# Sparse attention with four buffers; memory keys, part of the memory values and the convolution's norm inside its loop; all convolution taps ahead of the rotary step

## The chip, the cores and the metric

One core of one Trainium2 chip. The metric is the device time of one launch in microseconds. TensorE is called PE below, VectorE DVE, ScalarE ACT, GpSimd POOL, and SyncE, which starts most weight transfers, SP.

## The reference, cut to what matters

A first block (pooling and gated mixers, then latent attention) gives x, 512 tokens by 1024 features. The second block, on x and on 256 memory tokens, is:

```python
# h = rmsnorm(x); z = h @ w_in, split into a, b, q, k/v pairs and gate logits
u = a * sigmoid(b)                            # 512 channels
y = depthwise_conv(u, 31 taps, causal) + bias
conv = silu(layernorm(y))                     # 512 features
q_r, k_s, k_w = rotary of the first 16 of 64 dimensions
# 8 heads, 2 key groups; three branches, each with its own gate:
o_cmp = softmax(q . compressed keys) @ compressed values      # 31 blocks
o_slc = causal softmax(q_r . k_s) @ v_s       # all blocks are selected at 512 tokens
o_win = causal softmax(q_r . k_w) @ v_w       # the window is 512 tokens
x = x + concat(conv, g0*o_cmp + g1*o_slc + g2*o_win) @ w_out
mem_n = rmsnorm(mem)                          # 256 tokens
k = mem_n @ w_mem_k;  v = mem_n @ w_mem_v;  q = rmsnorm(x) @ w_mem_q
x = x + softmax(q . k / 16) @ v @ w_mem_o     # 4 heads
x = final_rmsnorm(x + peer(rmsnorm(x)))       # 128 gathered expert rows per token
```

## The kernel before, in words

Every engine runs one instruction list written out by hand, and the lists meet at semaphores. Activations lie feature-major (128 features on the partitions, tokens along a row). All is fp32. PSUM's eight banks are handed out ahead of time: each use of a bank is a job, `claim` waits for the bank's earlier use to be read out (`freed`), `done` and `full` tell that a result stands in it. Weights come in blocks of 1024 by 512 (2 MB) through a ring of three slots. SP walks the list `BLOCKS` (L39) in order and loads block b once block b-3 was released by PE (L452 to L475).

The change touches the stage of sparse attention and what lies around it, in this order on PE:

- Input projection (L786 to L807), block by block. Before the last two token tiles of its fifth block PE makes six products for the rotary step (L798, L801). DVE works on the convolution meanwhile: 124 instructions, 31 taps for each of 4 channel tiles (`conv_taps`, L1641; `CACC` is the sum). It does 92 of them (L1666), then the rotary step (L1669 to L1677: three instructions for each of six tiles, which frees six banks), and spreads the other 32 over the loop below (L1733).
- Compressed keys and values (L809 to L827). Their jobs take the banks that the rotary step frees. L830 waits for all six rotary tiles before the loop begins.
- The loop of sparse attention, 64 items: 8 heads, 4 query tiles `qt`, 2 branches. An item is 128 queries by (qt+1)*128 keys. PE makes the scores (`scores2`, L859, 64 rows of the array in use), DVE adds the mask, takes the maximum and its negative into `SM` (`masked_max`, L1706), ACT takes the exponential into `P2` (L1257), DVE divides by the sum and multiplies by the gate (`normalise`, L1578, its last instruction L1587), PE transposes (`transpose2`, L869), ACT copies out to `PT2` (L1263), and PE multiplies by the values (`values2`, L878). `SM`, `P2` and `PT2` have two buffers. Each head also has a small compressed branch (L832 to L857, L1678 to L1704).

The order in the loop before, per item i:

```python
PE:  scores2(i + 2); transpose2(i); values2(i - 1)
DVE: normalise(i); masked_max(i + 2); one convolution tap in 3 of 4 items
ACT: exp(i); copy_out(i - 1)
```

- In the loop ACT squares the memory tokens (item 4), PE sums them (item 10), and DVE scales them into `MEMT` (items 16 to 23).
- After the loop PE sums the convolution's channels (L914), makes the memory keys from `MEMT` in two blocks of 32 products of 256 columns (L917 to L921), with the sum of squares for the convolution's variance between them (L923), and waits for `mix_conv`: the SiLU of the normed convolution (L924, L1283 to L1286 on ACT), for which DVE centers, inverts and scales (L1753 to L1756).
- Then the output projection `out2` (L931), the memory values in two blocks of 16 products of 512 columns (L933 to L941), the memory queries, memory attention, and the expert stage, which gathers 512 rows of 8 KB per partition and takes the second half of the time.

Of the kernel before, what the change touches and what calls it, by code (L numbers as in the profile page):

```python
# [19 lines left out]
KC = D // P  # L20
# [7 lines left out]
TAPS = 31  # L28
# [11 lines left out]
          ("mem_k", 2), ("out2", 2), ("mem_v", 2), ("mem_q", 2), ("mem_o", 2), ("peer_q", 4)]  # L40
# [50 lines left out]
def build(nc, a, out):  # L91
# [8 lines left out]
    with ctx:  # L100
# [104 lines left out]
        SM = area(80, 2, L)  # L205
# [10 lines left out]
        P2 = area(72, 2, L)  # L216
        PT2 = area(76, 2, L)
        SB2 = area(169, 4, L)
        SQ2 = area(72, 4, L)
# [8 lines left out]
        MV = area(120, 2, D)  # L228
        MQ = area(128, KC, L)
# [169 lines left out]
        for hh in range(8):  # L399
            if hh % 2 == 0:  # L400
                j_o2[hh // 2] = J.take(6 + (hh // 2) % 2)
            j_cs[hh] = J.take(5)
            j_cpt[hh] = J.take(5)
            if hh == 1:
                j_rms_mem = [J.take(5)]
            for m in range(8):
                j_s2[8 * hh + m] = J.take((8 * hh + m) % 3)
                j_pt2[8 * hh + m] = J.take(3 + (8 * hh + m) % 2)
        J.align()
        j_ln_cv = [J.turn(1)]  # L410
        j_mk = J.turn(4)
        j_ln_cv.append(J.turn(1))
        j_mk += J.turn(4)
        j_rms_mq = J.turn(1)
        j_out2 = J.turn(8, [j_rms_mq[0][0]])
        j_mv = J.turn(4)
# [68 lines left out]
        def _(pe):  # L485
# [383 lines left out]
            def transpose2(i):  # L869
                hh, qt, br = ITEMS2[i]  # L870
                j = j_pt2[i]
                claim(pe, j)
                pe.wait_ge(S["p_ready"], N1 + i + 1)
                for kt in range(qt + 1):
                    ins = nc.tensor.transpose(bank(j, P, kt * P), P2[:, i % 2, kt * P:(kt + 1) * P], ident[:, :])  # L875
                done(ins, j)

            def values2(i):  # L878
                hh, qt, br = ITEMS2[i]
                jj, g = HEAD2[hh]  # L880
                jo = j_o2[hh // 2]
                read_out(pe, [j_pt2[i]])
                for kt in range(qt + 1):
                    ins = mm(bank(jo, P, qt * P, p0=64 * g, p1=64 * g + 64), VSW[:, kt, P * br + 64 * g:P * br + 64 * g + 64],  # L884
                             PT2[:, i % 2, kt * P:(kt + 1) * P], start=False, stop=(i % 8 == 7 and kt == qt))
                if i % 16 == 15:
                    done(ins, jo)
                    pe.wait_ge(bank_full[jo[0]], jo[1])
                    pe.sem_inc(S["pt_used"], 1)
                else:  # L890
                    ins.then_inc(S["pt_used"], 1)

            cmp_scores(0)
# [20 lines left out]
            norm_sum(j_ln_cv[0][0], CACC, 0, L, 4, S["conv_y"], 0)  # L914

            pe.wait_ge(S["mem_ready"], KC)
            for b in range(2):  # L917
                w = weights("mem_k", b)
                for c in range(4):
                    feat(j_mk[4 * b + c], w[:, c, :, :], MEMT, 0, LC)  # L920
                release_block(j_mk[4 * b + 3])  # L921
                if b == 0:
                    norm_sum(j_ln_cv[1][0], SQ2, 0, L, 4, S["squared"], 32)  # L923
# [9 lines left out]
            for b in range(2):  # L933
                w = weights("mem_v", b)
                for t in range(2):
                    j = j_mv[2 * b + t]
                    claim(pe, j)
                    for k in range(KC):
                        ins = mm(bank(j), MEMT[:, k, t * P:(t + 1) * P], w[:, :, k, :], start=(k == 0), stop=(k == KC - 1))  # L939
                    done(ins, j)  # L940
                release_block(j)  # L941
# [127 lines left out]
        def _(act):  # L1069
# [179 lines left out]

            for i in range(65):  # L1250
                if i < 64:
                    if i == 0:
                        cmp_exp(0)
                    n = (ITEMS2[i][1] + 1) * P
                    after(i, j_pt2)
                    act.wait_ge(S["p_max"], N1 + i + 1)
                    fn(P2[:, i % 2, 0:n], SM[:, i % 2, 0:n], ACT.Exp, bias=nmx[:, i % 8:i % 8 + 1], scale=0.125,  # L1257
                       accum_out=rsum[:, i % 8:i % 8 + 1]).then_inc(S["p_exp"], 1)
                if i >= 1:
                    n = (ITEMS2[i - 1][1] + 1) * P  # L1260
                    if i >= 3:
                        act.wait_ge(S["pt_used"], N1 + i - 2)
                    copy_out(j_pt2[i - 1], PT2[:, (i - 1) % 2, 0:n], n)  # L1263
                    if (i - 1) % 8 == 0:
                        cmp_pt((i - 1) // 8)
                    if i % 8 == 6 and i < 56:
                        cmp_exp(i // 8 + 1)
                    if i == 4:

                        act.wait_ge(S["mem_loaded"], 16)  # L1270
                        for k in range(KC):
                            fn(MEMSQ[:, k, :], MEMT[:, k, :], ACT.Square).then_inc(S["mem_sq"], 1)
                    if i == 12:
                        root(j_rms_mem[0], RSM[:, :], LC)

            squares(SQ2, CACC, 0, L, 4, S["centered"], 24)
            for c in range(4):
                copy_out(j_mk[c], MK[:, c, :], LC)
            root(j_ln_cv[1][0], RS2[:, :], L)  # L1280
            for c in range(4, 8):
                copy_out(j_mk[c], MK[:, c, :], LC)
            for c in range(4):  # L1283
                act.wait_ge(S["scaled"], 24 + c + 1)
                fn(CACC[:, c, :], CACC[:, c, :], ACT.Silu, bias=vc("conv_ln_b", c), scale=vc("conv_ln_g", c))\
                    .then_inc(S["mix_conv"], 1)  # L1286
# [4 lines left out]
            for b in range(2):  # L1291
                for t in range(2):
                    copy_out(j_mv[2 * b + t], MV[:, t, 512 * b:512 * b + 512])
# [99 lines left out]
        def _(dve):  # L1393
# [272 lines left out]
            conv_taps(4 * TAPS - 32)  # L1666
# [39 lines left out]
            def masked_max(i):  # L1706

                c, n, j = i % 8, (ITEMS2[i][1] + 1) * P, j_s2[i]
                full(dve, j)

                freed(v.tensor_tensor_reduce(out=SM[:, i % 2, 0:n], in0=bank(j, n), in1=MASK[:, L - n:L], scale=1.0, scalar=-3.0e38,  # L1712
                                             op0=ALU.add, op1=ALU.max, accum_out=mx[:, c:c + 1]), j)
                read_out(dve, [j])
                v.tensor_scalar(nmx[:, c:c + 1], mx[:, c:c + 1], -0.125, None, ALU.mult).then_inc(S["p_max"], 1)
# [6 lines left out]
            masked_max(1)  # L1722
            for i in range(64):
                hh, qt, br = ITEMS2[i]
                jj, g = HEAD2[hh]
                head = 4 * g + jj
                dve.wait_ge(S["p_exp"], i + 1)
                normalise(N1 + i, None, P2[:, i % 2, 0:(qt + 1) * P], gates_tok[:, qt, 3 * head + 1 + br:3 * head + 2 + br])
                if i + 2 < 64:
                    masked_max(i + 2)  # L1730
                if i % 8 == 5 and i < 56:
                    cmp_shift(hh + 1)
                if i % 4 < 3:  # L1733
                    conv_taps(1)

                if i == 11:
                    variance(j_rms_mem[0], D, LC)
                if i == 14:
                    inverse(RSM[:, :], LC)
                if 16 <= i < 16 + KC:  # L1740
                    k = i - 16
# [4 lines left out]
                if i % 16 == 1 and i > 1:  # L1746
                    j = j_o2[i // 16 - 1]
                    full(dve, j)
                    freed(v.tensor_copy(OATT[:, i // 16 - 1, :], bank(j)), j)
            j = j_o2[3]  # L1750
            full(dve, j)
            freed(v.tensor_copy(OATT[:, 3, :], bank(j)), j)
            dve.wait_ge(S["conv_y"], 4)  # L1753
            center(j_ln_cv[0][0], CACC, 0, L, 4, 512)
            invert(j_ln_cv[1][0], RS2[:, :], 512)
            scale(RS2[:, :], CACC, 0, L, 4)  # L1756
# [356 lines left out]
```

## Time and profile before

| | |
|---|---|
| median of 3 runs | 3013.92 us (3012.33 to 3015.02) |
| the profiled execution's own time | 3013.54 us |
| its span in the profile | 3011.7 us |
| time outside the span | 1.8 us |
| PE, DVE, ACT busy | 87%, 48%, 21% of the span |
| mean granted PE clock | 0.908 of full |

### The profile page before, as it was taken

How to read it: one execution, taken by the hardware profiler on the slowest of the kernel's cores; microseconds unless marked ns; L12 is line 12 of the kernel's file. 1: busy time of each engine (PE TensorE's matmuls, PEld its weight loads, DVE VectorE, ACT ScalarE, POOL GpSimd, SP SyncE). 2: the span in 40 equal slices, each digit the busy share in tenths (PEclk: the TensorE clock that was granted, in tenths of full speed). 3: DMA queues.
4: the chain of work that ended last, by engine and by line, in shares of the span. 5: the costliest groups of instructions: out<-in, count | busy, mean ns of one | idle time of the engine just before them, and what ended most of it. 6: DMA issues, size and time to landing. Idle time of an engine off the chain costs nothing.

```text
span 3011.7 us, 22314 instructions
## 1 busy us (share of the span) xinstructions
PE 2609.5 (87%) x7486; PEld 1262.9 (42%) x7486; DVE 1439.9 (48%) x3627; ACT 636.2 (21%) x1492; POOL 597.5 (20%) x554
## 2 busy tenths in 40 slices
PE   6999999899979989999999987877878787778876
PEld 2456544436534555554544433323333333333332
DVE  0002122135243764311114177777777777777774
ACT  2000012116221132211211122222221222222221
POOL 0000000000000000000000154444444444444442
PEclk8999899999989975599999999999898889898999
DMA  8101042200101200013113399999999999999996
GB/s 346 56 31 54 28 182 84 84 0 1 63 28 60 97 1 1 1 56 112 56 42 154 126 405 422 421 422 421 421 421 421 417 411 419 420 417 414 415 417 266
DMA packets 83154, 648.49 MB, mean 215 GB/s; under 512 B 9329, under 2 KB 9617, under 8 KB 10978
## 3 DMA queue, kind: packets, MB, share of 16 engines
q0 software_dynamic: 75696, 551.95, 44.4%
q1 hardware_dynamic: 7346, 95.12, 8.4%
q8 instruction: 62, 1.02, 0.1%
q14 instruction: 50, 0.41, 0.0%
HBM read 644.93 MB, written 2.10 MB: 215 GB/s over the span
## 4 chain that ended last, share of the span: by engine, by line
PE 59%; DMA 26%; DVE 8%; ACT 2%; issue 2%; POOL 1%; DVEq 0%; ACTq 0%; POOLq 0%; SPq 0%; PEldq 0%
PE psum L502 27%; DMA arena<-in_peer_uv,newton 25%; PE psum L1042 10%; PE psum L576 3%; PE psum L867 2%; PE psum L884 2%; DVE arena L1847 2%; PE psum L875 1%; PE psum L558 1%; PE psum L535 1%; PE psum L671 1%; PE psum L721 1%; PE psum L939 1%; PE psum L729 1%; DVE arena L1502 1%
## 5 line engine op out<-in xcount | busy, mean ns | idle before, releaser
L1042 PE MATMUL psum<-arena 128*128 128x512 f32 x2048 | 1009.2, 651 | 276.6 <-ACT arena L1348 276.2
L502 PE MATMUL psum<-arena 128*128 128x512 f32 (+2 forms) x2080 | 811.2, 550 | 26.8 <-DVE arena L1519 12.5
L1042 PEld LDWEIGHTS psum<-arena 128*128 128x128 f32 x2048 | 417.3, 209 | 866.6 <-issue 866.5
L1847 DVE CUSTOM_DVE_ANT_0 arena<-arena 128x1024 f32<-128x1024 f32 x512 | 620.7, 1224 | 323.8 <-DMA arena<-in_peer_uv,newton 319.8
L1974 POOL DMA_INDIRECT arena<-in_peer_uv,newton x512 | 566.9, 1107 | 892.4 <-PE psum L1042 733.5
L502 PEld LDWEIGHTS psum<-arena 128*128 128x128 f32 (+1 forms) x2080 | 395.1, 191 | 434.3 <-issue 411.4
L1074 ACT ACTIVATE arena<-psum 128x512 f32<-128x512 f32 (+8 forms) x335 | 177.5, 542 | 962.3 <-PE psum L502 505.8
L1348 ACT ACTIVATE arena<-ident,newton 128x128 f32<-128x128 f32 x512 | 165.0, 391 | 242.1 <-DVE newton L1855 228.2
L1339 ACT ACTIVATE arena<-arena 128x4 f32<-128x4 f32 x128 | 26.3, 205 | 706.9 <-DVE arena L1847 706.9
L1575 DVE TENSOR_REDUCE small<-psum 128x1 f32<-128x768 f32 (+1 forms) x48 | 37.5, 780 | 123.4 <-PE psum L955 85.0
L1905 POOL DMA_DIRECT2D arena<-in_sub_keys x1 | 0.5, 530 | 472.6 <-PE psum L975 472.6
L576 PE MATMUL psum<-arena 128*128 128x512 f32 x192 | 85.0, 605 | 5.1 <-DVE arena L1425 4.8
L1495 DVE TENSOR_SCALAR newton<-psum 128x512 f32<-128x512 f32 (+1 forms) x11 | 6.8, 617 | 169.2 <-PE psum L651 115.3
L867 PE MATMUL psum<-arena 64*128 64x128 f32 (+3 forms) x128 | 84.5, 762 | 0.0
L1712 DVE CUSTOM_DVE_ANT_0 arena<-psum,arena 128x128 f32<-128x128 f32 (+3 forms) x64 | 31.4, 491 | 108.9 <-PE psum L867 108.9
L1657 DVE SCALAR_TENSOR_TENSOR arena<-arena,vec 128x512 f32<-128x512 f32 x120 | 82.2, 737 | 0.0
L884 PE MATMUL psum<-arena 128*64 128x128 f32 x320 | 78.3, 405 | 0.0
L513 PE MATMUL psum<-arena,small 128*2 128x256 f32 x384 | 51.1, 426 | 26.9 <-DMA arena<-in_weights 25.6
L1116 ACT ACTIVATE arena<-arena 128x512 f32<-128x512 f32 (+1 forms) x36 | 18.9, 579 | 219.0 <-DVE arena L1485 218.9
L884 PEld LDWEIGHTS psum<-arena 128*64 128x64 f32 x320 | 54.6, 205 | 18.8 <-issue 18.5
L576 PEld LDWEIGHTS psum<-arena 128*128 128x128 f32 x192 | 37.1, 194 | 52.2 <-issue 47.4
L875 PE MATMUL psum<-ident,arena 128*128 128x128 f32 x160 | 48.0, 421 | 11.0 <-DVE arena L1587 11.0
(255 smaller groups left out, 1933.2 us busy)
## 6 DMA issues: line engine op xcount, KB each, us to landing
arena<-in_weights SPq DMA_DIRECT2D x44, 2048.0 KB, 8.4
arena<-in_peer_uv,newton POOLq DMA_INDIRECT x512
arena<-in_xin POOLq DMA_DIRECT2D x1, 3072.0 KB, 16.5
arena<-in_dft_l POOLq DMA_DIRECT2D x1, 2048.0 KB, 14.2
arena<-in_cmp_w POOLq DMA_DIRECT2D x1, 2048.0 KB, 7.6
out<-arena SPq DMA_DIRECT2D x4, 512.0 KB, 7.7
arena<-in_pool_band POOLq DMA_DIRECT2D x1, 1280.0 KB, 6.0
arena<-in_fnet_w POOLq DMA_DIRECT2D x1, 1024.0 KB, 20.9
```

What stands on the lines that cost most here:

```text
L502: ins = mm(bank(j, n, p1=m), w[:, k, 0:m], src[:, k, lo:lo + n], start=(k == 0), stop=(k == kc - 1))
L513: ins = mm(bank(jobs[b], 256, 256 * half, 64 * half, 64 * half + 2), cond[:, k, :], w[:, 2 * half:2 * half + 2, k, :], start=(k == 0), sto ...
L576: ins = mm(bank(j), H[:, k, t * P:(t + 1) * P], w[:, :, k, :], start=(k == 0), stop=(k == KC - 1))
L867: done(mm(bank(j, n), q, src[r:r + 64, 0:n], start=True, stop=True), j)
L875: ins = nc.tensor.transpose(bank(j, P, kt * P), P2[:, i % 2, kt * P:(kt + 1) * P], ident[:, :])
L884: ins = mm(bank(jo, P, qt * P, p0=64 * g, p1=64 * g + 64), VSW[:, kt, P * br + 64 * g:P * br + 64 * g + 64], PT2[:, i % 2, kt * P:(kt + 1) ...
L1042: ins = mm(bank(j_y[t][q]), DIAG[i % 4], ROW[ROW_PLACE[i]][:, D + 512 * q:D + 512 * q + 512], start=(r == 0), stop=(r == 127))
L1074: ins = fn(dst, bank(j, n, lo, p0, p1), func)
L1348: fn(DIAG[i % 4], ident[:, :], ACT.Copy, scale=GATES[:, n, e:e + 1]).then_inc(S["diag_ready"], 1)
L1657: ins = v.scalar_tensor_tensor(out=CACC[:, c, :], in0=src, scalar=w, in1=CACC[:, c, :], op0=ALU.mult, op1=ALU.add)
L1847: v.tensor_tensor_reduce(out=u, in0=u, in1=HNT[:, i // 128, :], scale=1.0, scalar=0.0, op0=ALU.mult, op1=ALU.add, accum_out=DOTS[:, i:i + ...
L1974: g.indirect_dma_start(out=ROW[ROW_PLACE[i]][:, :], out_offset=None, in_=a["peer_uv"], in_offset=bass.IndirectOffsetOnAxis(ap=IDX[:, n, e: ...
```

## The change

- The loop: `SM`, `P2` and `PT2` get four buffers; scores use two PSUM banks instead of three, so that a bank is free for the new products. Each engine's order becomes:

```python
PE:  scores2(i + 3); transpose2(i); values2(i - 2); memory_step(i)
DVE: masked_max(i + 3); normalise(i)
ACT: exp(i + 1); copy_out(i - 1)
```

- `memory_step(i)` makes two products of 256 columns of the memory keys in items 10 to 33 and 38 to 45 (all 64), and one product of 512 columns of the memory values' first block in items 46 to 61 (all 16). The second block of the values stays after `out2`. In `BLOCKS` the first values block goes ahead of `out2`.
- The convolution's norm goes into the loop: sums at items 34 and 41 on PE, center, variance, inverse and scaling at items 35, 42, 44 and 46 on DVE, squares, root and SiLU at items 37, 43 and 49 on ACT. The memory tokens' norm goes to items 1 to 13.
- All 124 convolution taps run before the rotary step; none is left in the loop.

```diff
-          ("mem_k", 2), ("out2", 2), ("mem_v", 2), ("mem_q", 2), ("mem_o", 2), ("peer_q", 4)]
+          ("mem_k", 2), ("mem_v_lo", 1), ("out2", 2), ("mem_v_hi", 1), ("mem_q", 2), ("mem_o", 2), ("peer_q", 4)]
...
-                j_s2[8 * hh + m] = J.take((8 * hh + m) % 3)
+                j_s2[8 * hh + m] = J.take((8 * hh + m) % 2)
...
+            def memory_step(i):
+                if 10 <= i < 34:
+                    n = i - 10
+                    memory_keys(n // 4, 2 * (n % 4), 2 * (n % 4) + 2)
+                elif 38 <= i < 46:
+                    n = i - 14
+                    memory_keys(n // 4, 2 * (n % 4), 2 * (n % 4) + 2)
+                elif 46 <= i < 62:
+                    n = i - 46
+                    memory_values(0, n // 8, n % 8, n % 8 + 1)
             cmp_scores(0)
-            for i in range(3):
+            for i in range(4):
                 scores2(i)
             for i in range(64):
-                if 1 <= i < 62:
-                    scores2(i + 2)
+                if 1 <= i < 61:
+                    scores2(i + 3)
                 transpose2(i)
                 if i % 8 == 0:
                     cmp_transpose(i // 8)
-                    if i:
-                        values2(i - 1)
+                if i >= 2:
+                    values2(i - 2)
+                if i % 8 == 1:
                     cmp_values(i // 8)
-                else:
-                    values2(i - 1)
                 if i % 8 == 4 and i < 56:
                     cmp_scores(i // 8 + 1)
-                if i == 10:
+                if i == 2:
                     norm_sum(j_rms_mem[0], MEMSQ, 0, LC, KC, S["mem_sq"], 0)
+                if i == 34:
+                    norm_sum(j_ln_cv[0][0], CACC, 0, L, 4, S["conv_y"], 0)
+                if i == 41:
+                    norm_sum(j_ln_cv[1][0], SQ2, 0, L, 4, S["squared"], 32)
+                memory_step(i)
...
-            conv_taps(4 * TAPS - 32)
+            conv_taps(4 * TAPS)
...
             masked_max(0)
             masked_max(1)
+            masked_max(2)
             for i in range(64):
...
+                if i + 3 < 64:
+                    masked_max(i + 3)
                 dve.wait_ge(S["p_exp"], i + 1)
-                normalise(N1 + i, None, P2[:, i % 2, 0:(qt + 1) * P], gates_tok[:, qt, 3 * head + 1 + br:3 * head + 2 + br])
-                if i + 2 < 64:
-                    masked_max(i + 2)
+                normalise(N1 + i, None, P2[:, i % 4, 0:(qt + 1) * P], gates_tok[:, qt, 3 * head + 1 + br:3 * head + 2 + br])
...
-                if i % 4 < 3:
-                    conv_taps(1)
```

## Rows read from the trace of the kernel before

**Rows 1.** The page: span, PE's busy time, granted PE clock in 40 slices.

```profile
span 3011.7 us, 22314 instructions
...
PE 2609.5 (87%) x7486; PEld 1262.9 (42%) x7486; DVE 1439.9 (48%) x3627; ACT 636.2 (21%) x1492; POOL 597.5 (20%) x554
...
PEclk8999899999989975599999999999898889898999
```

**Rows 2.** Busy time by stretch: loop start, loop, its long stretch, after it, memory values.

```profile
core 0: us, PE busy (x) PEld busy (x) DVE busy (x) ACT busy (x) POOL busy (x), PEclk, DMA share, GB/s
...
1041.70:1047.30 5.60, 2.96 (x14) 2.27 (x15) 3.36 (x17) 2.18 (x6) 0.00 (x0) 0.58 0.37 154
1047.30:1283.80 236.50, 226.42 (x722) 126.62 (x722) 115.24 (x417) 75.03 (x214) 0.00 (x0) 0.57 0.00 1
...
1110.80:1281.50 170.70, 168.64 (x495) 93.02 (x496) 77.47 (x289) 48.99 (x143) 0.00 (x0) 0.50 0.00 1
...
1283.80:1324.00 40.20, 34.97 (x144) 27.19 (x144) 11.93 (x15) 11.62 (x19) 0.00 (x0) 0.98 0.24 79
```

**Rows 3.** The same view, four whole heads of the loop.

```profile
1133.00:1257.00 124.00, 122.96 (x363) 67.77 (x362) 55.14 (x208) 35.24 (x104) 0.00 (x0) 0.50 0.00 1
```

**Rows 4.** Line L1587 (normalise's last instruction): who waited for it.

```profile
  PE psum L875: 11.0, 10
```

**Rows 5.** Timeline of DVE: masked_max and normalise back to back, dearest and cheapest pair.

```profile
1210.92 0.69 DVE L1712 CUSTOM_DVE_ANT_0 arena<-psum,arena 128x512 f32<-128x512 f32 x1 [2.33 <-PE psum L867]
...
1211.92 0.48 DVE L1587 TENSOR_SCALAR arena<-arena,small 128x384 f32<-128x384 f32 x1
...
1226.18 0.42 DVE L1712 CUSTOM_DVE_ANT_0 arena<-psum,arena 128x256 f32<-128x256 f32 x1 [1.98 <-PE psum L867]
...
1226.91 0.34 DVE L1587 TENSOR_SCALAR arena<-arena,small 128x128 f32<-128x128 f32 x1
```

**Rows 6.** Timeline of DVE, two instructions at the hand-offs with PE.

```profile
1087.56 0.56 DVE L1712 CUSTOM_DVE_ANT_0 arena<-psum,arena 128x384 f32<-128x384 f32 x1 [3.60 <-PE psum L867]
...
1095.25 0.55 DVE L1587 TENSOR_SCALAR arena<-arena,small 128x512 f32<-128x512 f32 x1
```

**Rows 7.** Timeline of PE in the loop: scores, and transposes that waited for DVE.

```profile
1086.61 0.91 PE L867 MATMUL psum<-arena 64*128 64x384 f32 x2
...
1095.94 0.63 PE L875 MATMUL psum<-ident,arena 128*128 128x128 f32 x4 [1.23 <-DVE arena L1587]
...
1100.82 1.09 PE L875 MATMUL psum<-ident,arena 128*128 128x128 f32 x4 [3.03 <-DVE arena L1587]
```

**Rows 8.** Timeline of PE after the loop: norm sum, memory keys, output projection, memory values.

```profile
1284.04 3.67 PE L558 MATMUL psum<-arena,ones 128*128 128x512 f32 x8 [0.30 <-PE psum L884]
1287.55 13.98 PE L502 MATMUL psum<-arena 128*128 128x256 f32 x64
...
1324.03 23.46 PE L502 MATMUL psum<-arena 128*128 128x512 f32 x48 [4.71 <-ACT arena L1285]
...
1389.30 13.90 PE L939 MATMUL psum<-arena 128*128 128x512 f32 x32
```

**Rows 9.** Timeline of DVE: taps ahead of the rotary step, rotary step, a reciprocal after the loop.

```profile
957.18 58.39 DVE L1657 SCALAR_TENSOR_TENSOR arena<-arena,vec 128x512 f32<-128x512 f32 x88
1017.35 0.69 DVE L1674 TENSOR_TENSOR arena<-psum,arena 128x512 f32<-128x512 f32 x1 [1.78 <-PE psum L798]
...
1029.70 0.69 DVE L1676 TENSOR_TENSOR arena<-arena 128x512 f32<-128x512 f32 x1
...
1306.99 3.35 DVE L1502 RECIPROCAL arena<-arena 128x512 f32<-128x512 f32 x1 [0.77 <-ACT arena L1121]
```

**Rows 10.** Timeline of PE: compressed keys, then the first products of the loop.

```profile
1032.01 7.36 PE L814 MATMUL psum<-arena 128*128 128x62 f32 x64
...
1041.70 1.26 PE L838 MATMUL psum<-arena 64*128 64x128 f32 x8 [0.61 <-issue]
```

**Rows 11.** DMA issues: the memory tokens' transfer, KB, and us to landing.

```profile
arena<-in_mem POOLq DMA_DIRECT2D x1, 1024.0 KB, 5.2
```

More of the change, by code:

```diff
@@ L204, in build @@
         MASK = area(153, L)
-        SM = area(80, 2, L)
+        SM = area(88, 4, L)
         CMASK = area(181.5, 4, 32)
@@ L215, in build @@
         PTC = area(188, L)
-        P2 = area(72, 2, L)
-        PT2 = area(76, 2, L)
+        P2 = area(72, 4, L)
+        PT2 = area(80, 4, L)
         SB2 = area(169, 4, L)
-        SQ2 = area(72, 4, L)
+        SQ2 = area(144, 4, L)
         TMP2 = area(156, 2, L)
@@ L227, in build @@
         MK = area(112, KC, LC)
-        MV = area(120, 2, D)
-        MQ = area(128, KC, L)
+        MV = area(136, 2, D)
+        MQ = area(96, KC, L)
         MO = area(144, KC, L)
@@ L403, in build @@
             j_cpt[hh] = J.take(5)
-            if hh == 1:
+            if hh == 0:
                 j_rms_mem = [J.take(5)]
+            if hh == 5:
+                j_ln_cv_var = J.take(5)
             for m in range(8):
-                j_s2[8 * hh + m] = J.take((8 * hh + m) % 3)
+                j_s2[8 * hh + m] = J.take((8 * hh + m) % 2)
                 j_pt2[8 * hh + m] = J.take(3 + (8 * hh + m) % 2)
+        j_mk = [J.take(2) for _ in range(6)]
+        j_ln_cv = [[J.take(2)], [j_ln_cv_var]]
+        j_mk += [J.take(2) for _ in range(2)]
+        j_mv = [J.take(2) for _ in range(2)]
         J.align()
[L410 to L413, printed above, removed]
         j_rms_mq = J.turn(1)
         j_out2 = J.turn(8, [j_rms_mq[0][0]])
-        j_mv = J.turn(4)
+        j_mv += J.turn(2)
         j_mq = J.turn(8)
@@ L874, in transpose2 @@
                 for kt in range(qt + 1):
-                    ins = nc.tensor.transpose(bank(j, P, kt * P), P2[:, i % 2, kt * P:(kt + 1) * P], ident[:, :])
+                    ins = nc.tensor.transpose(bank(j, P, kt * P), P2[:, i % 4, kt * P:(kt + 1) * P], ident[:, :])
                 done(ins, j)
@@ L884, in values2 @@
                     ins = mm(bank(jo, P, qt * P, p0=64 * g, p1=64 * g + 64), VSW[:, kt, P * br + 64 * g:P * br + 64 * g + 64],
-                             PT2[:, i % 2, kt * P:(kt + 1) * P], start=False, stop=(i % 8 == 7 and kt == qt))
+                             PT2[:, i % 4, kt * P:(kt + 1) * P], start=False, stop=(i % 8 == 7 and kt == qt))
                 if i % 16 == 15:
@@ L891, in values2, with memory_keys, memory_values @@
                     ins.then_inc(S["pt_used"], 1)
+            def memory_keys(c, first, last):
+                w = weights("mem_k", c // 4)
+                j = j_mk[c]
+                for k in range(first, last):
+                    if k == 0:
+                        claim(pe, j)
+                    pe.wait_ge(S["mem_ready"], k + 1)
+                    ins = mm(bank(j, LC), w[:, c % 4, k, :], MEMT[:, k, :], start=(k == 0), stop=(k == KC - 1))
+                if last == KC:
+                    done(ins, j)
+                    if c % 4 == 3:
+                        release_block(j)
+            def memory_values(b, t, first, last):
+                w = weights(("mem_v_lo", "mem_v_hi")[b], 0)
+                j = j_mv[2 * b + t]
+                for k in range(first, last):
+                    if k == 0:
+                        claim(pe, j)
+                    ins = mm(bank(j), MEMT[:, k, t * P:(t + 1) * P], w[:, :, k, :], start=(k == 0), stop=(k == KC - 1))
+                if last == KC:
+                    done(ins, j)
+                    if t == 1:
+                        release_block(j)
+            def memory_step(i):
[8 more added lines that the diff above has]
+                    memory_values(0, n // 8, n % 8, n % 8 + 1)
             cmp_scores(0)
-            for i in range(3):
+            for i in range(4):
                 scores2(i)
             for i in range(64):
-                if 1 <= i < 62:
-                    scores2(i + 2)
+                if 1 <= i < 61:
+                    scores2(i + 3)
                 transpose2(i)
@@ L901, in _ @@
                     cmp_transpose(i // 8)
-                    if i:
-                        values2(i - 1)
+                if i >= 2:
+                    values2(i - 2)
+                if i % 8 == 1:
                     cmp_values(i // 8)
-                else:
-                    values2(i - 1)
                 if i % 8 == 4 and i < 56:
                     cmp_scores(i // 8 + 1)
-                if i == 10:
+                if i == 2:
                     norm_sum(j_rms_mem[0], MEMSQ, 0, LC, KC, S["mem_sq"], 0)
-            values2(63)
[L914 to L923, printed above, removed]
+                if i == 34:
[3 more added lines that the diff above has]
+                memory_step(i)
+            values2(62)
+            values2(63)
             pe.wait_ge(S["mix_conv"], 4)
@@ L931, in _ @@
             output("out2", j_out2, MIX3, SEGS[:1], mq_sum)
[L933 to L941, printed above, removed]
+            for t in range(2):
+                memory_values(1, t, 0, KC)
             pe.wait_ge(S["h_ready"], 32)
@@ L1247, in cmp_pt, with exp2 @@
                 copy_out(j_cpt[hh], PTC[0:N_CMP, :], p1=N_CMP)
-            for i in range(65):
[L1251 to L1258, printed above, removed]
+            def exp2(i):
+                n = (ITEMS2[i][1] + 1) * P
+                if i >= 4:
+                    full(act, j_pt2[i - 4])
+                act.wait_ge(S["p_max"], N1 + i + 1)
+                fn(P2[:, i % 4, 0:n], SM[:, i % 4, 0:n], ACT.Exp, bias=nmx[:, i % 8:i % 8 + 1], scale=0.125,
+                   accum_out=rsum[:, i % 8:i % 8 + 1]).then_inc(S["p_exp"], 1)
@@ L1259, in _, with transposed2 @@
+            def transposed2(i):
+                n = (ITEMS2[i][1] + 1) * P
+                if i >= 4:
+                    act.wait_ge(S["pt_used"], N1 + i - 3)
+                copy_out(j_pt2[i], PT2[:, i % 4, 0:n], n)
+            cmp_exp(0)
+            exp2(0)
+            for i in range(65):
+                if i + 1 < 64:
+                    exp2(i + 1)
                 if i >= 1:
-                    n = (ITEMS2[i - 1][1] + 1) * P
-                    if i >= 3:
-                        act.wait_ge(S["pt_used"], N1 + i - 2)
@@ L1263, in _ @@
-                    copy_out(j_pt2[i - 1], PT2[:, (i - 1) % 2, 0:n], n)
+                    transposed2(i - 1)
                     if (i - 1) % 8 == 0:
                         cmp_pt((i - 1) // 8)
[L1266 to L1286, printed above, removed]
+                if i % 8 == 6 and i < 56:
+                    cmp_exp(i // 8 + 1)
@@ new lines, in _ @@
+                if i == 1:
+                    act.wait_ge(S["mem_loaded"], 16)
+                    for k in range(KC):
+                        fn(MEMSQ[:, k, :], MEMT[:, k, :], ACT.Square).then_inc(S["mem_sq"], 1)
+                if i == 4:
+                    root(j_rms_mem[0], RSM[:, :], LC)
+                if i in (14, 18, 22, 26, 30, 34):
+                    copy_out(j_mk[i // 4 - 3], MK[:, i // 4 - 3, :], LC)
+                if i == 37:
+                    squares(SQ2, CACC, 0, L, 4, S["centered"], 24)
@@ new lines, in _ @@
+                if i in (42, 46):
+                    copy_out(j_mk[i // 4 - 4], MK[:, i // 4 - 4, :], LC)
+                if i == 43:
+                    root(j_ln_cv[1][0], RS2[:, :], L)
+                if i in (54, 62):
+                    copy_out(j_mv[(i - 54) // 8], MV[:, (i - 54) // 8, 0:512])
+                if i == 49:
+                    for c in range(4):
+                        act.wait_ge(S["scaled"], 24 + c + 1)
+                        fn(CACC[:, c, :], CACC[:, c, :], ACT.Silu, bias=vc("conv_ln_b", c), scale=vc("conv_ln_g", c))\
+                            .then_inc(S["mix_conv"], 1)
@@ L1290, in _ @@
             root(j_rms_mq[0], RS2[:, :], L)
-            for b in range(2):
-                for t in range(2):
-                    copy_out(j_mv[2 * b + t], MV[:, t, 512 * b:512 * b + 512])
+            for t in range(2):
+                copy_out(j_mv[2 + t], MV[:, t, 512:D])
             for c in range(8):
@@ L1709, in masked_max @@
                 full(dve, j)
-                freed(v.tensor_tensor_reduce(out=SM[:, i % 2, 0:n], in0=bank(j, n), in1=MASK[:, L - n:L], scale=1.0, scalar=-3.0e38,
+                freed(v.tensor_tensor_reduce(out=SM[:, i % 4, 0:n], in0=bank(j, n), in1=MASK[:, L - n:L], scale=1.0, scalar=-3.0e38,
                                              op0=ALU.add, op1=ALU.max, accum_out=mx[:, c:c + 1]), j)
@@ L1726, in _ @@
                 head = 4 * g + jj
+                if i + 3 < 64:
+                    masked_max(i + 3)
                 dve.wait_ge(S["p_exp"], i + 1)
[L1728 to L1730 removed]
+                normalise(N1 + i, None, P2[:, i % 4, 0:(qt + 1) * P], gates_tok[:, qt, 3 * head + 1 + br:3 * head + 2 + br])
                 if i % 8 == 5 and i < 56:
                     cmp_shift(hh + 1)
[L1733 to L1736 removed]
+                if i == 3:
                     variance(j_rms_mem[0], D, LC)
[L1738 removed]
+                if i == 5:
                     inverse(RSM[:, :], LC)
[L1740 to L1741 removed]
+                if 6 <= i < 6 + KC:
+                    k = i - 6
                     v.scalar_tensor_tensor(out=MEMT[:, k, :], in0=MEMT[:, k, :], scalar=vc("memkv_g", k), in1=RSM[:, :],
@@ L1745, in _ @@
                     cmp_normalise(hh + 1)
-                if i % 16 == 1 and i > 1:
+                if i % 16 == 3 and i > 3:
                     j = j_o2[i // 16 - 1]
@@ L1749, in _ @@
                     freed(v.tensor_copy(OATT[:, i // 16 - 1, :], bank(j)), j)
+                if i == 35:
+                    dve.wait_ge(S["conv_y"], 4)
+                    center(j_ln_cv[0][0], CACC, 0, L, 4, 512)
+                if i == 42:
+                    variance(j_ln_cv[1][0], 512, L)
+                if i == 44:
+                    inverse(RS2[:, :], L)
+                if i == 46:
+                    scale(RS2[:, :], CACC, 0, L, 4)
             j = j_o2[3]
@@ L1752, in _ @@
             freed(v.tensor_copy(OATT[:, 3, :], bank(j)), j)
[L1753 to L1756, printed above, removed]
             for c in range(8):
@@ L2056 @@
                         pad(np.concatenate([kv2[3], kv2[5], w2[:, 2304:2328]], axis=1), 512)], axis=1),
-        i["w_mem_k_2"][0],
+        i["w_mem_k_2"][0], i["w_mem_v_2"][0][:, 0:512],
         np.concatenate([out2[0:512]] + [out2[512 + 64 * h:576 + 64 * h] for h in heads], axis=0),
-        i["w_mem_v_2"][0], i["w_mem_q_2"][0], i["w_mem_o_2"][0], i["peer_w_q_2"][0],
+        i["w_mem_v_2"][0][:, 512:D], i["w_mem_q_2"][0], i["w_mem_o_2"][0], i["peer_w_q_2"][0],
     ]
```

## The prediction

> **What bounds the kernel now.** I read the page first, for the clock of each slice, then busy time by stretch around the loop, then who waits for whom in it, and last the timelines. PE is busy 87% of the span at full clock nearly everywhere, except in the slices of the sparse loop [rows 1]. Its 236.5 us have a mean granted clock of 0.57, and from 1110.8 to 1281.5 us PE is at the lower level (1.2 GHz) throughout although it is busy 168.6 of 170.7 us [rows 2]. So PE bounds the loop there, at half speed: four heads take 124.0 us with PE busy 122.96 and DVE 55 [rows 3]. A head costs 31.0 us of PE at half clock, about 15.5 at full. PE's waits for normalise sum to only 11.0 us, in 10 items of 64 [rows 4]: the order of before (normalise, then the next maximum) keeps DVE one item ahead. After the loop PE runs at 0.98, 34.97 of 40.2 us busy [rows 2].
>
> The points to move are: the loop 242.1 us (1041.7 to 1283.8), the stretch to `out2` 40.2 us, the first values block 13.9 us [rows 2, 8].
>
> **Taps ahead of the rotary step.** A tap takes 58.39 / 88 = 0.664 us, so 32 more take 21.2 us. The taps ended at 1015.57, as DVE then waited 1.78 us for PE; the rotary step now starts at 1036.8 instead of 1017.35 and, 13.0 us long, ends at 1049.9 [rows 9]. The compressed keys' first bank comes free with the first rotary tile at 1039.0 (they began at 1032.0), and with their 9.7 us up to the loop they would be done at 1048.7. The rotary end sets it: the loop starts at 1050.1 instead of 1041.7 [rows 10], **+8.4 us**. In the loop DVE loses 21 us of work that cost nothing where PE was the bound [rows 3].
>
> **The new order in the loop.** This decides. On PE `scores2(i+3)` stands right ahead of `transpose2(i)`. On DVE `masked_max(i+3)` now stands ahead of `normalise(i)`. The transpose needs the normalise, that stands behind the maximum, and that needs the scores which PE has just made. Each item is then a chain PE, DVE, PE, and four buffers don't loosen it, as no buffer is what is waited for. Behind PE's wait stand the values, the memory step and the next scores; ACT and DVE wait for those. The DVE leg: from the start of the maximum to the end of normalise 1211.92 + 0.48 - 1210.92 = 1.48 us for the dearest pair (512 and 384 keys), 1226.91 + 0.34 - 1226.18 = 1.07 us for the cheapest; mean 1.28 [rows 5]. Hand-offs: scores end at 1087.52, the maximum starts at 1087.56; normalise ends at 1095.80, the transpose starts at 1095.94 [rows 6, 7]; 0.18 together. So 1.46 us for each of 60 items (1 to 60): **88 us** in which PE stands still, at either clock. Before, this was 11.
>
> **PE's own work in the loop.** Eight heads: 248 us at half, 124 at full. Added to them: memory keys 2 x 13.98, first values block 13.9, two sums 2 x 3.67 [rows 8], and the memory tokens' sum, a quarter of a key block, 3.5: 52.7 at full, 105 at half. Together 177 at full, 353 at half. The loop's start, before the first transpose, stays 5.6 [rows 2].
>
> **DVE blocks between items.** An inverse of 512 columns is 3.35 + 3 x 0.69 = 5.4 us [rows 9], against some 2.8 us of PE's work in an item at full clock: 2.6 late. Center, scaling and the memory's inverse are about half as long: I take 5 us for all at full clock, none at half (above them: 10 if all are late). ACT's moved squares, roots and copies lie beside the 1.46 us waits: nothing, or some 5 us without that cover. The memory tokens land 5.2 us after issue [rows 11]; they are issued behind the same product as before, and item 1 comes some 7 us into the loop: nothing, up to 5 if late.
>
> **The clock.** Loop at full clock throughout: 177 + 88 + 6 + 5 = 276 us; at half throughout: 353 + 88 + 6 = 447. The trace has no stretch like the new one, so I bound it by these. Against full clock: a transpose at 1100.82 came behind a 3.03 us wait and its four instructions took 1.09 us, against 0.63 at 1095.94 [rows 7], so the clock had fallen there; it fell for good at 1110.8 [rows 2]; and the new loop adds a wait to every item. For it: the stretches with full-array products hold 0.98 [rows 2], and items 10 to 61 get them. Items 0 to 9 have almost none, and I put them at half: 23 us more, 299. Of the other 154 us of work I put half at each level, midway as neither row is near: +77. The loop is **376 us**, 134 more than before.
>
> A rule from the Trainium skill, "TensorE: Matmul & The Clock Gate", Part 1 (the HAM clock gate), says that the engine is slow by default and that sustained activity releases it. By it a PE that is busy 98.8% of 170.7 us should have run at full clock; the trace disagrees, with 0.50. With the page's reading the loop would be the 276 us above.
>
> **After the loop.** Of the 40.2 us to `out2`, the copy of the last head pair's outputs stays, about 0.9: **-39.3**. This includes the 4.71 us wait for the SiLU [rows 8]; SiLU stands at item 49, far ahead. The first values block goes: 13.9 and the 0.3 hand-off, **-14.2**. The same weight blocks are loaded; `out2` waits behind the release of the keys in the loop, hundreds of us ahead of need, and the second values block comes behind item 61 with all of `out2` (65 us) to cover it, then the queries' blocks as before: nothing. If that cover failed, one block's transfer would show there.
>
> **The sum.** +8.4 + 134 - 39.3 - 14.2 = +89 us on the profiled execution's own 3013.54 (the median is 3013.92, 0.4 more): **3102 us**. All else moves along. The change pays once the new loop takes less than 242 + 39.3 + 14.2 - 8.4 = 287 us.
>
> **Rivals.**
> 1. Full clock all through, by the page's rule: loop 276, 11 us gained, 3002. For it: dense products. Against: 0.50 over 170.7 us with PE busy. This is the rival on the other side; it decides if fewer than about 11 us of the 177 us work run at half. Chance 0.05.
> 2. The waits are hidden after all, since four buffers give slack that I miss: loop 177 + 23 + 11 = 211, 2937. Against: all three lists are in order. Chance 0.03. This is also the case in which my chain is not in the code.
> 3. The dense products hold full clock from item 10 on: loop 299, +12, 3025; with a tenth of it low, up to 3045. Chance 0.12.
> 4. The waits hold the clock low to the end: loop 447, +160, 3173. For it: each item adds a wait to a loop that already sat low. Chance 0.10.
>
> The forecast has 0.70. Its own range is 3050 to 3150 (15 to 80% of the work at half). Taking rival 3 in, 3030 to 3155 holds 8 in 10. A measurement of this kernel can tell about 0.2% from no change, 6 us: faster 0.08 (1 and 2), same 0.02, slower 0.90.
>
> **What would show it.** Right: transposes wait for normalise in nearly every item, 1.1 to 1.5 us each, 80 to 100 us in sum; the maximum starts right behind the scores, and DVE's chain through L1712 and L1587 is on the path; the loop starts 8 us later; `out2` follows the loop within 1 us; 16 values products after `out2`. Wrong: few such waits (rival 2), a granted clock of 1.0 (3) or 0.5 (4) from item 10 on, or a loop under 287 us.

## The result, and the profile after

The changed kernel takes 3147.19 us (median of 4 runs, 3135.58 to 3157.86) against 3014.47 (4 runs): 1.0439 times, 95% interval 1.0387 to 1.0491. The runs of the changed kernel stand in two pairs 22 us apart, at a mean granted clock of 0.897 and 0.898 in one and 0.886 and 0.889 in the other; the profiled one is the fastest, 3135.58 us, 122 us over the profiled one of before.

The page of the changed kernel, two lines that answer to [rows 1]:

```profile
PE 2644.5 (84%) x7486; PEld 1273.3 (41%) x7486; DVE 1439.6 (46%) x3627; ACT 636.6 (20%) x1494; POOL 598.7 (19%) x554
...
PEclk9998989999989657757999998989989999989999
```

PE runs the same number of instructions, 7486, and is busy 35 us longer: more of them at half clock. Busy time of the changed kernel's loop (columns: stretch, its length, busy time and instructions of PE, PEld, DVE, ACT, POOL, then the granted clock, DMA share and GB/s):

```profile
1056.10:1462.60 406.50, 313.21 (x912) 169.14 (x912) 108.29 (x414) 90.65 (x243) 0.00 (x0) 0.63 0.04 16
```

The loop takes 406.5 us where it took 242.1. Who waited for normalise's last instruction (L1625 in the changed kernel):

```profile
  PE psum L877: 89.6, 61
```

That was 11.0 us in 10 items [rows 4]. The timeline of the changed kernel, one item late in the loop, DVE and PE together, shows the chain that answers to [rows 5 to 7]:

```profile
1440.94 2.07 PE L869 MATMUL psum<-arena 64*128 64x512 f32 x2
1443.05 0.69 DVE L1750 CUSTOM_DVE_ANT_0 arena<-psum,arena 128x512 f32<-128x512 f32 x1 [5.47 <-PE psum L869]
...
1444.05 0.41 DVE L1625 TENSOR_SCALAR arena<-arena,small 128x256 f32<-128x256 f32 x1
...
1444.61 0.66 PE L877 MATMUL psum<-ident,arena 128*128 128x128 f32 x2 [1.59 <-DVE arena L1625]
```

The scores end at 1443.01, the maximum starts at 1443.05, normalise ends at 1444.46 and the transpose starts at 1444.61. DVE had been idle for 5.47 us before the maximum: it did nothing until the scores came, and PE did nothing until DVE was through. The 61 waits above say that nearly every item looks so.

PE's timeline around the loop of the changed kernel:

```profile
1039.27 13.91 PE L816 MATMUL psum<-arena 128*128 128x62 f32 x64 [6.99 <-DVE arena L1714]
...
1463.53 20.84 PE L504 MATMUL psum<-arena 128*128 128x512 f32 x48 [0.94 <-DVE arena L1797]
...
1526.18 13.90 PE L916 MATMUL psum<-arena 128*128 128x512 f32 x32
```

| Stage | before, us | after, us | difference |
|---|---|---|---|
| start of the loop | 1041.7 | 1056.1 | +14.4 |
| the loop | 242.1 | 406.5 | +164.4 |
| loop end to `out2` | 40.2 | 0.9 | -39.3 |
| `out2`, to the values block behind it | 65.3 | 62.7 | -2.6 |
| memory values behind `out2` | 28.2 | 14.2 | -14.0 |

The sum is +122.9, the spans differ by 122.1 (3133.8 against 3011.7). The whole loss is in the loop and just ahead of it.

### The profile page after: what moved, and what is told of

Same layout as the page of the kernel before. It is cut to its first block, busy times and chain, and to the rows that moved or that the text cites. A ratio compares the mean times of both kernels' runs of the same rounds, so it can differ in the third digit from the quotient of the medians.

```text
span 3133.8 us, 22345 instructions
## 1 busy us (share of the span) xinstructions
PE 2644.5 (84%) x7486; PEld 1273.3 (41%) x7486; DVE 1439.6 (46%) x3627; ACT 636.6 (20%) x1494; POOL 598.7 (19%) x554
## 4 chain that ended last, share of the span: by engine, by line
PE 57%; DMA 24%; DVE 12%; issue 2%; ACT 2%; POOL 1%; DVEq 0%; ACTq 0%; POOLq 0%; SPq 0%; PEldq 0%
DMA arena<-in_peer_uv,newton 24%; PE psum L504 23%; PE psum L1070 10%; PE psum L578 3%; DVE arena L1695 3%; PE psum L869 2%; PE psum L886 2%; PE psum L903 2%; DVE arena L1888 2%; PE psum L916 1%; PE psum L560 1%; PE psum L877 1%; PE psum L537 1%; PE psum L673 1%; DVE arena L1750 1%
## 5 line engine op out<-in xcount | busy, mean ns | idle before, releaser
L504 PE MATMUL psum<-arena 128*128 128x512 f32 (+2 forms) x1952 | 781.4, 560 | 23.2 <-DVE arena L1557 12.5
L504 PEld LDWEIGHTS psum<-arena 128*128 128x128 f32 (+1 forms) x1952 | 370.3, 191 | 425.0 <-issue 410.5
L1102 ACT ACTIVATE arena<-psum 128x512 f32<-128x512 f32 (+9 forms) x335 | 177.4, 542 | 1081.4 <-PE psum L504 485.7
L877 PE MATMUL psum<-ident,arena 128*128 128x128 f32 x160 | 43.2, 387 | 89.9 <-DVE arena L1625 89.6
L877 PEld LDWEIGHTS psum<-ident,arena 128*128 128x128 f32 x160 | 24.2, 189 | 137.3 <-issue 137.3
L869 PE MATMUL psum<-arena 64*128 64x128 f32 (+3 forms) x128 | 75.0, 683 | 2.4 <-DVE small L1750 2.1
L886 PE MATMUL psum<-arena 128*64 128x128 f32 x320 | 70.2, 372 | 0.0
```

Of the source, the lines that this page charges most:

```text
L504: ins = mm(bank(j, n, p1=m), w[:, k, 0:m], src[:, k, lo:lo + n], start=(k == 0), stop=(k == kc - 1))
L869: done(mm(bank(j, n), q, src[r:r + 64, 0:n], start=True, stop=True), j)
L877: ins = nc.tensor.transpose(bank(j, P, kt * P), P2[:, i % 4, kt * P:(kt + 1) * P], ident[:, :])
L1102: ins = fn(dst, bank(j, n, lo, p0, p1), func)
```

## The experiments

My theory, as predicted: each item is a chain through PE, DVE and PE, because `masked_max(i + 3)` stands ahead of `normalise(i)`; the wait costs its own length and keeps the clock low. The rivals were the work moved into the loop (at half clock there), scores with two banks instead of three, DVE's load, and the taps. All loop lengths and waits below are from one profile each; that of the changed kernel is of its faster pair of runs.

**Normalise first.** The changed kernel with two statements of DVE's loop swapped:

```diff
-                if i + 3 < 64:
-                    masked_max(i + 3)
                 dve.wait_ge(S["p_exp"], i + 1)
                 normalise(...)
+                if i + 3 < 64:
+                    masked_max(i + 3)
```

> The changed kernel with the old order on DVE alone: normalise(i) ahead of masked_max(i + 3). Theory (the chain PE, DVE, PE in each item is the loss): PE's waits for normalise fall from 89.6 us to under 20, the loop from 406 to 230 to 260 us, the time to 2955 to 2995 us. Rival (the loop is slow because of the work moved into it, which runs at half clock there, or because scores have two banks instead of three): the waits go but PE's work fills them, the loop stays over 300 us and the time over 3030 us.

Measured: 2965.79 us (2964.93 to 2969.48), 0.984 of before (0.9824 to 0.9856). Its loop, and who waited for normalise:

```profile
1056.60:1293.90 237.30, 222.17 (x912) 127.02 (x912) 108.37 (x414) 93.04 (x243) 0.00 (x0) 0.88 0.08 26
...
  PE psum L877: 11.2, 5
```

The same 912 PE instructions take 237 us instead of 406. The moved work, the two score banks, the norms and the taps are all still there, so none of them makes the loop slow without the order. (What the norms still cost is shown further down.) The waits fell by 78.4 us, the loop by 169.2: the other 90.8 us are PE's own work (busy 222 us instead of 313), at a clock of 0.88 instead of 0.63.

**The same swap in the kernel before.** Nothing else of the change is in this kernel.

```diff
                 dve.wait_ge(S["p_exp"], i + 1)
-                normalise(...)
                 if i + 2 < 64:
                     masked_max(i + 2)
+                normalise(...)
```

> The kernel before with one line moved: masked_max(i + 2) ahead of normalise(i), nothing else. Theory: the wait of 1.1 to 1.8 us appears in some 60 items there too, 80 to 90 us of waits instead of 11, and with a loop as slow in clock as before the time is 3085 to 3115 us. Rival (the order matters little, the moved work does): within 10 us of 3014.

Measured: 3109.04 us (3106.89 to 3115.23), 1.0318 of before (1.0301 to 1.0336). Its loop, its waits, and one of the waits in PE's timeline:

```profile
1041.10:1378.70 337.60, 238.63 (x736) 134.23 (x736) 118.71 (x432) 75.56 (x220) 0.00 (x0) 0.54 0.01 3
...
  PE psum L875: 97.3, 62
...
1206.74 1.09 PE L875 MATMUL psum<-ident,arena 128*128 128x128 f32 x4 [1.43 <-DVE arena L1587]
```

The order alone makes most of the loss: 95 of 133 us. 86.3 us more of waits cost 95.5 us of loop here, hardly more than their length; this loop was at half clock for most of its time anyway (0.57 before, 0.54 now). In the loop with the memory products, 78.4 us of waits cost 169.2.

**One more instruction, in the chain and behind it.** A sum of 512 columns that nobody reads, in items 1 to 60 of the changed kernel:

```diff
                 if i + 3 < 64:
                     masked_max(i + 3)
+                if 1 <= i <= 60:                       # first kernel: here
+                    link(v.tensor_tensor(ANG[:, :], MASK[:, :], MASK[:, :], ALU.add))
                 dve.wait_ge(S["p_exp"], i + 1)
                 normalise(...)
+                                                       # second kernel: the same two lines here
```

> The changed kernel with one more DVE instruction (a sum of 512 columns, 0.73 us from start to start, its result unused) between masked_max(i + 3) and normalise(i) in items 1 to 60. Theory: it lies in each item's chain, so PE's waits grow by 60 x 0.73 = 44 us to about 134, and the time by at least that, more if the clock falls further: 3185 to 3225 us. Rival (DVE's load as a whole sets the pace, or the loop's time is clock alone): the same time as its twin that has the instruction behind normalise.

> The twin: the same extra instruction behind normalise(i). Theory: it lies beside PE's transposes, values and memory step (1.5 us or more), so the waits stay at about 90 us and the time at 3125 to 3165 us. Rival: as slow as the kernel with the instruction ahead of normalise.

Measured: 3199.15 us (3196.07 to 3199.56) in the chain, 3149.88 (3148.30 to 3152.36) behind it. The loop and the waits with the instruction in the chain:

```profile
1054.90:1523.40 468.50, 332.40 (x912) 180.53 (x912) 149.87 (x474) 90.94 (x243) 0.00 (x0) 0.60 0.04 13
...
  PE psum L877: 132.4, 61
```

and behind it:

```profile
1055.20:1475.60 420.40, 321.79 (x912) 172.78 (x912) 146.88 (x474) 91.38 (x243) 0.00 (x0) 0.61 0.04 15
...
  PE psum L877: 94.9, 61
```

DVE is busy about the same 150 and 147 us in both. Behind normalise the extra 39 us of DVE work leave the time where the changed kernel's runs lie (3135.58 to 3157.86); the profiled loop is 13.9 us longer. In the chain the waits grow by 42.8 us, 60 times 0.71, and the loop by 62.0. Against its twin, which has the same instructions in another order, the waits are 37.5 us more, the loop 48.1 and the time 49.3. So DVE's load is not what hurts; its place is.

**The memory step in the wait.** The changed kernel with PE's list altered and DVE's order left as it is:

```diff
                     scores2(i + 3)
+                memory_step(i)
                 transpose2(i)
...
-                memory_step(i)
```

> The changed kernel with memory_step(i) between scores2(i + 3) and transpose2(i) on PE, that is in the wait, and not behind the values; DVE's order as changed. Theory: the 48 steps (0.9 us at full clock, 1.7 at half) cover the wait in their items; the waits fall from 90 to 20 to 45 us, and with some more time at full clock the total is 3050 to 3095 us. Rival (the wait is on something that follows PE's work, so moving work into it only moves the wait): 3125 to 3160 us.

Measured: 3006.53 us (10 runs, 3004.78 to 3010.82), 0.9979 of before (0.9969 to 0.9989). Its loop and waits:

```profile
1056.00:1333.80 277.80, 231.73 (x912) 131.15 (x912) 108.35 (x414) 89.34 (x243) 0.00 (x0) 0.84 0.07 24
...
  PE psum L877: 39.9, 52
```

The waits came out as expected, the time 44 us below the expected range. 49.7 us less of waits took 128.7 us off the loop, since the clock rose from 0.63 to 0.84. A chain needs not be broken: independent work between the two hand-offs fills it.

**All memory products behind the loop.** With normalise first, the 64 key products and 16 value products stand between the loop and `out2`, with their copies on ACT and their PSUM banks moved too:

```diff
-                memory_step(i)
             values2(62)
             values2(63)
+            for c in range(8):
+                memory_keys(c, 0, KC)
+            for t in range(2):
+                memory_values(0, t, 0, KC)
```

> Normalise first, as in the fast version, but all memory products that the change put into the loop stand behind it, ahead of out2. This asks why 42 us of products cost nothing in that loop. Theory (they lift the granted clock): without them the loop is at half clock for most of its length, as before, and takes 240 to 255 us; with the products behind it the time is 3010 to 3035 us. Rival (the deeper buffers made the loop faster by themselves): the loop takes 195 to 205 us and the time is about 2966 us.

Measured: 2988.52 us (2986.84 to 2989.30). Neither held: the loop takes 216 us, between the two. Busy time of this loop, of a stretch at full clock and of one at half:

```profile
1056.60:1272.80 216.20, 195.67 (x752) 112.51 (x752) 107.76 (x415) 88.44 (x233) 0.00 (x0) 0.75 0.01 4
1098.00:1169.70 71.70, 63.55 (x310) 35.11 (x309) 43.02 (x173) 30.54 (x87) 0.00 (x0) 1.00 0.00 1
1203.80:1268.70 64.90, 62.96 (x181) 34.47 (x181) 27.91 (x108) 23.58 (x59) 0.00 (x0) 0.50 0.00 1
```

The loop with four buffers and no memory products holds full clock for 71.7 us without interruption. It falls to half at the end of a wait for normalise of 3.05 us, comes back 17 us later without any memory product, and falls again in a wait of 4.86 us. It then stays at half for 64.9 us though PE is busy 63.0 of them. With the products (normalise first) the loop is at 0.88 and this last stay at half is 9 us long, behind a wait of 3.60 us; 42 us of products make the loop only 21.1 us longer. The clock of the two loops differs in little else, so what the products save is most of that last stay.

This loop is 26 us shorter than the one of before, at a clock of 0.75 instead of 0.57, and fewer waits are not the reason: PE waits 17.3 us for normalise in it, against 11.0. The missing taps are not the reason either (the kernel before without them in its loop, under "The taps", takes 241.2 us there). Four buffers, two score banks and the look-ahead of three items were not tried one by one.

**Where the clock falls.** This is read from the version with normalise first, without a run of its own. Three of its five waits for normalise are 10.5 of the 11.2 us:

```profile
1087.72 0.99 PE L877 MATMUL psum<-ident,arena 128*128 128x128 f32 x4 [3.87 <-DVE arena L1625]
...
1191.06 0.87 PE L877 MATMUL psum<-ident,arena 128*128 128x128 f32 x3 [3.05 <-DVE arena L1625]
...
1232.59 0.88 PE L877 MATMUL psum<-ident,arena 128*128 128x128 f32 x3 [3.60 <-DVE arena L1625]
```

Ahead of each of them DVE is busy with a norm that the change put into the loop: the inverse for the memory tokens (item 5), the centering (item 35) and the inverse for the convolution (item 44). At each the granted clock goes from 1.00 to 0.50, for 10, 15 and 9 us; from 1098.0 to 1190.4 and from 1241.5 us to the loop's end it is 1.00. The kernel before shows the same at its own inverse: 0.99 in the last 0.8 us of the 3.03 us wait, 0.50 in the 3.4 us behind it [rows 7]. So the moved norms do have a price in this loop. That these waits bring the clock down is told by the order in time alone: no run here has the norms in shorter pieces or elsewhere.

**The taps.** The changed kernel with 92 taps ahead and one in each of items 0 to 31; and the kernel before with all 124 ahead:

```diff
-            conv_taps(4 * TAPS)
+            conv_taps(4 * TAPS - 32)
...
                 normalise(...)
+                conv_taps(1)
```

> The changed kernel with 92 taps ahead of the rotary step and the other 32 in items 0 to 31 of the loop, behind normalise. Theory: the loop starts at about 1042 us as before instead of 1056, the taps lie beside PE's transposes and values, and the time falls by about 14 us, to 3120 to 3145 us. Rival (DVE in the loop is what hurts): 32 x 0.66 = 21 us more in the loop, and the time is the same or over 3147 us.

> The kernel before with all 124 taps ahead of the rotary step and none in the loop. Theory: the loop starts 8 to 14 us later (compressed keys wait for the rotary step, and may run at half clock), and nothing comes back, as PE is the bound in the loop: 3020 to 3030 us. Rival (DVE relief pays in the loop): 3014 or less.

Measured: 3120.74 us (3114.00 to 3128.58) and 3028.69 us (3026.40 to 3030.22; 1.0047 of before, 1.0030 to 1.0063). The first loop starts at 1041.4 and takes 399.9 us with 90.3 us of waits, so 32 taps in it cost nothing there and the rival is out. The second starts at 1055.4 and takes 241.2. From the second kernel's timeline of PE:

```profile
1038.54 13.91 PE L814 MATMUL psum<-arena 128*128 128x62 f32 x64 [7.01 <-DVE arena L1676]
```

The 64 products took 7.36 us before [rows 10]. PE waits 7.0 us for the rotary step to free a bank and then runs them at a granted clock of 0.50 (1.00 before). That is the taps' cost: the loop starts 13.7 us later in this kernel and gives 0.9 us back.

**A version that beats both.** Normalise first with taps given back to the loop. First 32 in items 0 to 31, then 16 in items 16 to 31, behind the items with the memory tokens' norm:

```diff
-            conv_taps(4 * TAPS)
+            conv_taps(4 * TAPS - 16)
...
+                if i >= 16:
+                    conv_taps(1)
```

> Normalise first, and 92 taps ahead of the rotary step with the other 32 in items 0 to 31: both repairs together. Theory: the two are independent; the loop starts at 1042 us instead of 1056 and takes the 237 us it took with normalise first, so 2966 falls to 2945 to 2958 us. Rival (once PE runs at full clock, the taps are late for the chain): waits for normalise grow from 11 to over 25 us, the clock falls, and the time is 2966 us or more.

> The same with 108 taps ahead and 16 in the loop, in items 16 to 31, where DVE has no norm of the memory tokens to do. By the rows of before the rotary step could start some 10 us later without PE waiting for it at the compressed keys or at the loop, so 16 more taps ahead cost nothing. Theory: loop start within 2 us of 1042, and fewer waits than with 32 taps in the loop: the same as its twin or up to 10 us faster, 2940 to 2955 us. Rival (the rotary step was already at its edge): the loop starts at 1050 us or later, and the time is over 2958 us.

Measured: 2963.36 us (5 runs, 2954.89 to 2968.09) with 32, and 2951.13 us (5 runs, 2950.02 to 2953.82) with 16, 0.9791 of before (0.9778 to 0.9805). With 32 the loop starts at 1041.1 but takes 247.8 us at a clock of 0.86; the waits are 13.2 us, not over 25, and the time lies between the two expectations. With 16:

```profile
1041.80:1276.40 234.60, 218.11 (x912) 124.42 (x912) 118.70 (x430) 92.92 (x243) 0.00 (x0) 0.90 0.08 28
```

The waits are 12.5 us, so hardly fewer. The two versions differ most behind the memory tokens' inverse: with 32 taps PE waits 4.53 us there and the clock is at 0.50 for the next 26.0 us, with 16 it waits 3.87 us and the clock is at 0.50 for 11.5. Why the one stay is longer was not settled. The loop starts where it did before, so 16 more taps ahead of the rotary step were free and 32 were not. This is the fastest of all, 12 us under its twin: 63.6 us below before, 196 below the changed kernel.

## Why the prediction was right

The direction, the chain and the range (3030 to 3155, against 3147) were right; the point, 3102, was 45 us low. Of these, 12 us lie between the profiled run and the median; the profile itself differs by 34: taps +6.0, loop +30.4, `out2` -2.6. By its own steps:

- **The new order.** Right, and by itself most of the loss: 61 waits of 89.6 us in sum against 60 and 88, with hand-offs of 0.04 and 0.15 us. The swap in the kernel before shows that it acts alone, the swap back that the change pays without it, the extra instruction that it is the place in the chain that counts.
- **Taps ahead.** Mis-sized: +14.4 instead of +8.4. I let the compressed keys take their 9.7 us from the first free bank and end before the rotary step. That step ended at 1050.1 us, where I had put 1049.9. But the 64 products behind the wait for the bank ran at a granted clock of 0.50 and took 13.91 us, so that they set the loop's start and not the rotary step. Taps in the loop cost nothing before, as said.
- **The clock.** This term was mis-sized most. I put 10 items and half of the other 154 us of PE's work at half clock, 100 of 177 us, and the loop at 376 us. It was 406.5. Less 89.6 of waits and 8.4 to the first transpose, 308.5 us remain for 177 us of work, so about 131 us of it, 74%, ran at half clock; the loop's granted clock of 0.63 says the same. With items 0 to 9 taken at half as I put them, that is about 70% of the 154 us, inside the 15 to 80% of the forecast. "Midway as neither row is near" was no measurement, and that the range still held owes something to its width. The memory products did not hold the clock up in a loop with a wait in each item.
- **DVE blocks between items.** I took 5 us at full clock, 10 if all are late. In the changed kernel they don't show apart: PE is idle 93.3 us in the loop, 89.6 of them for normalise. With normalise first, mostly at full clock, they are three waits of 10.5 us in sum, and the clock falls at each; the prediction had no price for that.
- **The loop's start** was 8.4 us to the first transpose, not 5.6: the scores of item 3 and the maxima of items 2 and 3 come ahead of it as well, PE waits 2.11 us for a maximum there, and the clock is at 0.50.
- **After the loop.** Right: 39.3 (39.3) and 14.0 (14.2). `out2` gained another 2.6 us, since it is at full clock from its start now (20.84 us for 48 products; 23.46 before, at 0.89 [rows 8]).
- **The Trainium skill's rule.** The page "TensorE: Matmul & The Clock Gate" of the Trainium skill, Part 1, has sustained activity release the clock. No run here was at full clock throughout the loop. In the version with the memory products behind, PE was busy 97% of the 64.9 us at half clock and 89% of the 71.7 us at full clock, so its busy time in these profiles does not say which level holds.
- **Rival 3** (dense products hold full clock from item 10 on) did not come about here. With normalise first the loop comes near it: 237 us at 0.88. Most of the value of the change was there; one order of two statements hid it.

## What to carry to other kernels

When two in-order engines pass work back and forth, draw the chain through both lists: a maximum for item i+3 put ahead of item i's last step ties the two items together, with two buffers between them and with four. Put the step that the other engine waits for first, the look-ahead behind it; or put independent work between the two hand-offs. Price a wait on PE by the clock it takes with it, not by its length, and remember that the products behind a long wait can run at half clock: here 64 of them took 13.91 us instead of 7.36 behind a wait of 7.0 us.

## What the runs showed of the hardware that was not expected

- A wait on PE cost between 1.1 and 2.6 times its length. In a loop that is at half clock anyway, 86.3 us of waits cost 95.5; in the changed kernel 42.8 more cost 62.0; taking away 78.4 gave 169.2, and 49.7 gave 128.7. These are differences between single profiles, and the changed kernel's own runs lie 22 us apart, so the factors are rough.
- One loop without memory products ran 71.7 us on end at full clock and 64.9 us at half, in items of the same kinds; the second stretch begins in a wait of 4.86 us.
- One kernel's runs can stand in two groups, each with its own clock: 3136 and 3158 us at 0.897 to 0.898 and 0.886 to 0.889. With the long chain of waits gone the spread was 4.5 us with all taps ahead, 3.8 with 16 in the loop and 13.2 with 32.
